# First expert weights and expert products in one block, with loads asked for early, staged inputs and one-hots in sets of two

## What is computed

```python
def peer(h, w_pq, sub_keys1, sub_keys2, u_table, v_table):
    ...
        q = (xb @ w_pq).reshape(PEER_BLOCK, PEER_HEADS, PEER_QDIM)
        ...
        v1, i1 = lax.top_k(s1, PEER_TOPK)
        v2, i2 = lax.top_k(s2, PEER_TOPK)
        ...
        top_s, sel = lax.top_k(cand, PEER_TOPK)
        eidx = jnp.take_along_axis(cidx, sel, axis=-1)
        g = jax.nn.softmax(top_s, axis=-1).astype(xb.dtype)
        act = jax.nn.gelu(jnp.einsum('thkd,td->thk', u_table[eidx], xb), approximate=False)
        return jnp.einsum('thk,thkd->td', g * act, v_table[eidx])
```

## Time and profile before

| | |
|---|---|
| Device time, median of 3 runs | 4201.07 us (4199.33 to 4202.46) |
| Time of the profiled execution | 4197.49 us |
| Its span, first to last instruction | 4195.7 us |
| TensorE busy | 3802.9 us, 91% |
| VectorE busy | 2992.6 us, 71% |
| ScalarE busy | 1232.7 us, 29% |
| GpSimd busy | 1747.3 us, 42% |
| Granted TensorE clock, mean | 0.932 of full speed |

### The profile page before, as it was taken

One profiled execution on the slowest core, in us unless ns is written; L12 is line 12 of the kernel. 1 busy time (PEld: TensorE's weight loads), 2 busy tenths in 40 slices (PEclk: granted clock), 3 DMA queues, 4 the chain that ended last, 5 costly groups with the idle time before them and its releaser, 6 DMA issues.

```text
span 4195.7 us, 58772 instructions
## 1 busy us (share of the span) xinstructions
PE 3802.9 (91%) x19146; PEld 3082.0 (73%) x19146; DVE 2992.6 (71%) x6028; ACT 1232.7 (29%) x1871; POOL 1747.3 (42%) x1065
## 2 busy tenths in 40 slices
PE   8899876999668999387999999999989999999998
PEld 1699843566555444166999999999979999999997
DVE  0322244333441999897999999998888888888888
ACT  0411033222222222074333333333223232332332
POOL 0222000000220233202565565555557777777775
PEclk9799977899779999657999999999999999999999
DMA  7388700566433111047999999999999999999997
GB/s 248 114 269 286 250 2 20 161 202 205 139 111 97 35 35 35 15 180 278 328 339 333 327 339 327 346 327 354 336 336 338 343 333 345 336 341 345 331 347 273
DMA packets 302319, 1018.03 MB, mean 243 GB/s; under 512 B 30394, under 2 KB 61916, under 8 KB 294932
## 3 DMA queue, kind: packets, MB, share of 16 engines
q1 hardware_dynamic: 155348, 489.04, 34.8%
q0 software_dynamic: 127584, 481.35, 31.5%
q10 hardware_dynamic: 19296, 46.67, 2.9%
...
## 4 chain that ended last, share of the span: by engine, by line
PE 52%; DVE 1%; DMA 0%; issue 0%; ACT 0%; DVEq 0%; POOLq 0%
PE p_y L2144 25%; PE p_a L2125 9%; PE p_a L2124 9%; PE p_a L2128 8%; PE next_pw L1752 2%; DMA h_lo<-h_spill 0%; DVE p_y L2110 0%; DVE h_lo L2096 0%; DVE rows L2066 0%; DVE h_rows L2079 0%; DVE h_rows L2102 0%; DVE h_hi L2094 0%; DVE x1g L2113 0%; ACT pairsT L1986 0%; DVE u_raw L2105 0%
## 5 line engine op out<-in xcount | busy, mean ns | idle before, releaser
L2013 POOL DMA_INDIRECT rows<-in_v,pairsT x384 | 763.2, 1987 | 276.3 <-DVE h_rows L2079 184.4
L2013 POOL DMA_INDIRECT rows<-u_rows,pairsT x384 | 632.9, 1648 | 477.0 <-DVE pairsT L2066 404.5
L2124 PE MATMUL p_a<-h_hi,u_hi 128*128 128x384 f32 x2048 | 688.7, 336 | 39.3 <-DVE h_lo L2096 38.0
L2125 PE MATMUL p_a<-h_lo,u_hi 128*128 128x384 f32 x2048 | 692.1, 338 | 0.0
L2144 PE MATMUL p_y<-v_hi,g_hi 128*128 128x512 f32 x1536 | 486.9, 398 | 0.0
L1981 ACT ACTIVATE v_hi<-v_raw 128x1024 fp32r<-128x1024 f32 x256 | 272.0, 1062 | 727.0 <-PE p_y L2144 714.1
L2144 PE MATMUL p_y<-v_lo,g_hi 128*128 128x512 f32 x1536 | 475.8, 391 | 0.0
L2079 DVE SCALAR_TENSOR_TENSOR h_rows<-rows,pairsT,h_rows 128x1024 f32<-128x1024 f32 x381 | 466.4, 1279 | 2.1 <-DMA rows<-in_v,pairsT 2.1
L2066 DVE CUSTOM_DVE_ANT_0 rows<-rows,h_rows 128x1024 f32<-128x1024 f32 x384 | 450.6, 1220 | 24.1 <-DMA rows<-u_rows,pairsT 23.9
L2124 PEld LDWEIGHTS p_a<-h_hi,u_hi 128*128 128x128 f32 x2048 | 386.2, 189 | 50.4 <-DVE h_lo L2096 38.7
L2128 PE MATMUL p_a<-h_hi,u_lo 128*128 128x384 f32 x2048 | 396.8, 334 | 0.5 <-DVE u_lo L2041 0.5
...
## 6 DMA issues: line engine op xcount, KB each, us to landing
...
```

Of the source, the lines that this page charges most:

```text
L2013: pool.indirect_dma_start(rows[s][n % SLOTS][:], None, (keep.u_rows, v_rows)[g], at).then_inc(rows_in[s][n % SLOTS], 16)
L2124: nc.tensor.matmul(p_a[:, 0:GT], u_hi[s][:, k, :], h_hi[:, k, :], start=k == 0, stop=False)
L2125: nc.tensor.matmul(p_a[:, 0:GT], u_hi[s][:, k, :], h_lo[:, k, :], start=False, stop=False)
```

## The change

- `stage_weights` is gone. Its steps run at the start of the block of `stage_experts`: SP first asks for `h_cols` (now in the `x1` buffers), then for `u` and `v` of `j` = 0 and 1, then stores the weight blocks; POOL first asks for `h_lo`, then the first six gathers, waits for all stores, and loads `w_ring` and `x1`; ScalarE makes the four splits and `h_hi` of the first group ahead of the weight steps; VectorE makes `h_lo` behind them. PSUM tiles are shared: the indices' and `h`'s transposes lie in `p_y`, the second bank of the weight steps is `p_a`.
- The input of the second group is loaded in turn 104 of the first to `h_next`, in the memory of `wt`, and split on VectorE right behind the last `weigh` of the first group.
- The last up product of a group finishes tile by tile (`y_tile`); VectorE multiplies each into `y` (`finished`), also in the memory of `wt`, so `p_y` is free for the next group after the multiplications; the additions (`added`) for the first group come in turn 2 of the second, their stores in turn 4 and the loads of `x1` for the second in turn 16, all on POOL's queue.
- Two ranks instead of one are treated in turns 4 and 8 of each group (`ranks_after`), so none is left behind the last turn.
- The one-hots of four tokens lie as two sets of two: `[set, key, token]` in place of `[key, token]`. VectorE's operations keep their number and size; TensorE reads one number in two.
- In `stage_scores` the sum of squares and the root stay ahead of `mix_columns`, the scaling goes behind it.

```diff
 
-            def norm(t):
+            def squares(t):
                 act.wait_ge(x1_full, t + 1)
 
                 nc.scalar.activation(xn[:], x1[:], ACT.Square, accum_out=st[:, 0:1]).then_inc(ss, 1)
                 act.wait_ge(ss, t + 1)
                 nc.scalar.activation(st[:, 1:2], st[:, 0:1], ACT.Sqrt, scale=1.0 / D, bias=keep.cols[:, 4:5]).then_inc(rms, 1)
+
+            def scaled(t):
                 act.wait_ge(rec, t + 1)
                 nc.scalar.activation(xn[:], x1[:], ACT.Copy, scale=st[:, 2:3]).then_inc(xn_full, 1)
 
@@ -1566,7 +1568,8 @@
             def before():
                 mix_columns(0)
                 mix_columns(1)
...
@@ -1578,9 +1581,11 @@
                 if not isinstance(t, int) or t >= 2:
                     exps(t - 2)
                 if projects:
-                    norm(t + 1)
+                    squares(t + 1)
                 if transposes:
                     mix_columns(t + 2)
+                if projects:
+                    scaled(t + 1)
...
-    B = 4
+    B, IN = 4, 2
+    SETS = B // IN
     STEPS = GROUP * P // B
     PER_BLOCK = BLOCK // B
-
-    def __init__(self, nc, sem, m, keep, banks, name, base, iota):
+    LEAD = 2
+
...
+        self.hot_i = [m.sb(f"hot_i{i}", [P, self.SETS, N_KEYS, self.IN], F16) for i in range(2)]
+        self.hot_j = [m.sb(f"hot_j{i}", [P, self.SETS, N_KEYS, self.IN], F16) for i in range(2)]
+        self.hot_w = [[m.sb(f"hot_w{i}{k}", [P, self.SETS, N_KEYS, self.IN], F16) for k in range(2)] for i in range(2)]
...
     def vector(self, dve, n, s):
 
         nc, keep = self.nc, self.keep
-        shape = [P, N_KEYS, self.B]
-        column = lambda x: x[:, bass.ds(n * self.B + self.base, self.B)].unsqueeze(1).to_broadcast(shape)
+        shape = [P, self.SETS, N_KEYS, self.IN]
+        column = lambda x: x[:, bass.ds(n * self.B, self.B)].rearrange("p (c b) -> p c b", b=self.IN).unsqueeze(2).to_broadcast(shape)
+        keys = self.iota.unsqueeze(1).to_broadcast(shape)
         dve.wait_ge(self.pw_full, n + 1)
-        nc.vector.tensor_tensor(self.hot_j[s][:], self.iota, column(keep.index[:, 1]), ALU.is_equal).then_inc(self.equal_full, 1)
-        nc.vector.tensor_tensor(self.hot_i[s][:], self.iota, column(keep.index[:, 0]), ALU.is_equal)
+        nc.vector.tensor_tensor(self.hot_j[s][:], keys, column(keep.index[:, 1]), ALU.is_equal).then_inc(self.equal_full, 1)
+        nc.vector.tensor_tensor(self.hot_i[s][:], keys, column(keep.index[:, 0]), ALU.is_equal)
         dve.wait_ge(self.equal_full, n + 1)
         for k in range(2):
             last = nc.vector.tensor_tensor(self.hot_w[s][k][:], self.hot_j[s][:], column(keep.parts[:, k]), ALU.mult)
         last.then_inc(self.hot_full, 1)
-    def tensor(self, pe, n, s):
+    def tensor(self, pe, n, s, banks):
+
         pe.wait_ge(self.hot_full, n + 1)
-        pe.wait_ge(self.pw_read, n + 1)
+        pe.wait_ge(self.pw_read, n + (self.LEAD + 1 - len(banks)))
...
+                last = self.nc.tensor.matmul(banks[s % len(banks)][:, b, :], self.hot_i[s][:, b // self.IN, :, b % self.IN],
+                                             self.hot_w[s][k][:, b // self.IN, :, b % self.IN], start=k == 0, stop=k == 1)
...
+    def store(self, eng, block, stored, ahead=0):
+
+        wait_count(eng, stored, (block - ahead) * 16)
         eng.sem_inc(self.wt_free, 1)
-        eng.wait_ge(self.pw_read, block * self.PER_BLOCK + (self.PER_BLOCK + self.banks))
+        eng.wait_ge(self.pw_read, block * self.PER_BLOCK + (self.PER_BLOCK + self.LEAD))
+        eng.dma_start(self.keep.w_dram[block], self.wt[:, block % 2]).then_inc(stored, 16)
...
+    wt_flat = w.wt[:].rearrange("p a k t -> p (a k t)")
+    h_next = wt_flat[:, 0:KD * GT].rearrange("p (k t) -> p k t", k=KD)
+    y = [wt_flat[:, i * D:(i + 1) * D] for i in range(GROUP)]
+    hs = [x1[s][:].rearrange("p (k c) -> p k c", k=KD) for s in range(SPARSE)]
+    pw = m.ps("pw", [P, w.B, N_KEYS])
+    one_bank = [pw[:]]
+    two_banks = [pw[:], p_a[:].rearrange("p (b k) -> p b k", b=w.B)]
+    p_idx = [p_y[0][:, 0, 0:DENSE_AT], p_y[0][:, 1, 0:DENSE_AT], p_y[1][:, 0, 0:DENSE_AT]]
+    p_h = p_y[2][:].rearrange("p b c -> p (b c)")
...
+    def ranks_after(j):
+
+        return min(J, j + 1 + (j >= 4) + (j >= 8))
+
+    def weight_steps(eng, body):
+        body(0, 0)
+        body(1, 1)
+        with eng.Fori(1, w.STEPS // 2) as k:
+            for s in range(2):
+                body(k * 2 + s, s)
+
...
-        rest(J - 2)
-        rest(J - 1)
...
+                def first():
+                    if g == 0:
+                        w.store(sp, 0, w.stored)
+                        with sp.Fori(1, BLOCKS) as b:
+                            w.store(sp, b, w.stored)
+
+                blocks(sp, g, load, lambda n, j, s: None, first)
...
+                def first():
+                    if g == 0:
+                        act.wait_ge(h_in, 16)
+                        nc.scalar.activation(h_hi[:], h_lo[:].bitcast(F32), ACT.Copy).then_inc(h_hi_full, 1)
+                        weight_steps(act, lambda n, s: w.scalar(act, n, s, two_banks))
...
+            def load_x1(g):
+                for i in range(GROUP):
+                    wait_count(pool, y_out[0][i], 16 * g)
+                    pool.dma_start(x1[i][:], keep.x1_dram[SPARSE + g * GROUP + i]).then_inc(x1_in[i], 16)
+
+            pool.dma_start(h_lo[:].bitcast(F32), keep.h2_dram[:, :, DENSE_AT:DENSE_AT + GT]).then_inc(h_in, 16)
+            pool.wait_ge(idx_done, 2)
...
+                for j in range(SLOTS):
+                    gather(g, j)
+                if g == 0:
+                    pool.wait_ge(w.stored, 16 * BLOCKS)
                 load_w(g, 0)
                 load_w(g, 1)
-
-                o = g * J
-                for j in range(SLOTS):
-                    gather(o + j)
+                if g == 0:
+                    pool.wait_ge(cols_turned, SPARSE)
+                    load_x1(0)
+                asked = SLOTS
                 for j in range(J):
-                    if j + SLOTS < J:
-                        gather(o + j + SLOTS)
+                    for n in range(asked, min(ranks_after(j) + SLOTS, J)):
+                        gather(g, n)
+                    asked = max(asked, min(ranks_after(j) + SLOTS, J))
                     if g < GROUPS - 1 and j < w.STEPS and j % w.PER_BLOCK == w.PER_BLOCK - 1:
-                        w.store(pool, j // w.PER_BLOCK)
+                        w.store(pool, j // w.PER_BLOCK + BLOCKS, w.stored_next, BLOCKS)
                     if j % JC == JC - 1 and j // JC + 2 < CHUNKS:
                         load_w(g, j // JC + 2)
+                    if g == 0 and j == w.STEPS + 8:
+                        pool.wait_ge(w.stored_next, 16 * BLOCKS)
+                        pool.dma_start(h_next, keep.h2_dram[:, :, DENSE_AT + GT:DENSE_AT + 2 * GT]).then_inc(h_in, 16)
+                    if g and j == 4:
+                        for i in range(GROUP):
+                            pool.wait_ge(y_full, i + 1)
+                            pool.dma_start(out_rows(SPARSE + i), x1[i][:]).then_inc(y_out[0][i], 16)
+                    if g and j == 16:
+                        load_x1(1)
...
+            def finished(g, i):
+                dve.wait_ge(y_tile, g * GROUP + i + 1)
+                nc.vector.tensor_mul(y[i], p_y[i][:].rearrange("p b c -> p (b c)"), keep.gate[:, 1, 1, :]).then_inc(y_mul, 1)
+
+            def added(g, i):
+                t = g * GROUP + i
+                dve.wait_ge(y_mul, t + 1)
+                dve.wait_ge(x1_in[i], 16 * (g + 1))
+                nc.vector.tensor_add(x1[i][:], x1[i][:], y[i]).then_inc(y_full, 1)
+
             for g in range(GROUPS):
+                def rest(j):
+                    for n in range(ranks_after(j - 1) if j else 0, ranks_after(j)):
+                        (dots, sums)[g](n)
+                    split_v(g * J + j + 2, j % 2)
+                    if g and j == 2:
+                        for i in range(GROUP):
+                            added(0, i)
+
+                def first():
+                    if g:
+                        dve.wait_ge(h_lo_full, g + 1)
+                        for i in range(GROUP):
+                            finished(0, i)
+                    split_v(g * J + 1, 1)
+
                 def between():
                     if g:
                         dve.wait_ge(rows_gelu, 1)
                         nc.vector.tensor_mul(keep.shares, keep.shares, keep.dots).then_inc(sums_done, 1)
                         dve.wait_ge(sums_done, 1)
 
-                def rest(j):
-                    (dots, sums)[g](j)
-                    if j + 2 < J:
-                        split_v(g * J + j + 2, j % 2)
-
-                dve.wait_ge(h_in, 16 * (g + 1))
-                nc.vector.tensor_copy(h_hi[:], h_lo[:].bitcast(F32)).then_inc(h_hi_full, 1)
+                raw = h_next if g else h_lo[:].bitcast(F32)
+                if g:
+                    dve.wait_ge(h_in, 32)
```

(40 more changed lines are left out.)

219 lines of the change are left out of this document (93 added, 126 removed).

## The result

| | before | after |
|---|---|---|
| Device time, median | 4201.76 us (4199.33 to 4202.82) | 4169.16 us (4161.68 to 4175.61) |
| Ratio after / before | | 0.9923 (95%: 0.9904 to 0.9942) |
| Profiled execution, time / span | 4197.49 / 4195.7 us | 4165.70 / 4163.9 us |
| TensorE, VectorE busy | 91%, 71% | 90%, 71% |
| Granted clock, mean | 0.932 | 0.933 |

A forecast was written before the change was run, and what follows sets the result against it. TensorE's down and up products bound the kernel: 4197.5 - 7 (block) - 15 (between groups) - 5 (end) + 3 (doubled ranks) - 35 (sets) = 4138.5 profiled, 4142 as median. Range 4127 to 4179.

The forecast's parts named there:

- Sets of two: One-hots in the weighted turns: fp16 products at 0.064 us, turn from 9.24 to 8.88 us, 35 us saved (0 to 40).
- rival (a): Weighted turns: reading is not what the fp16 products pay for, 35 of 59 us fall away, 4177; chance 0.28.
- The stops: Weighted turns of the first group: 3 us of stop, 0 to 7, from two ranks in turns 4 and 8.
- rival (b): Weighted turns: VectorE or the DMA engines hold the turn at 9.0 to 9.1 us, 4155 to 4165; chance 0.12.
- The doubled ranks: Turns 4 and 8: 3.4 us more VectorE work each; 3 us of stop in the first group, second group's lead covers it.
- The block: Weights and experts as one block: TensorE starts at about 1928, 7 us saved at the first up product (2 to 14).
- the first weights: Stage building the first weights: VectorE is the bound, so the one-hots in sets gain nothing there.
- rival (d): Block's start: loads, gathers and stores make the first eviction late, eating the whole hand-over; 4149; inside the forecast's chance 0.53.
- Between the groups: Hand-over from first to second group: TensorE's stop goes and the clock stays, 15 us saved (12 to 17).
- the end: Kernel's end: sparse sums done before, closing operations wait only for loads; 5 us saved (0 to 6).
- the scaling: Late scaling in the score stage: VectorE is the bound there, so 0 us saved (to 2).
- the likeliest case: Whole kernel: all terms as forecast, 4142 us; forecast band 4126 to 4154, with (d) in it, chance 0.53.

The follow-up runs named there:

- the pieces: The changed kernel with each 1.5 MB load of w_ring cut into six of 0.25 MB, one in each of six turns: 4142.10 us, ratio 0.9858.

## Why the prediction was right in its range and short in its size

**Sets of two: right, and a little better.** The turn was forecast at 8.88 us, it is 8.84. TensorE's price was put at 64 ns a product on the line of the 4-byte steps; it is 57 to 58. The three steps that are now measured at full clock are 118 ns (8 bytes), 57 (4 bytes) and 56 (2 bytes). At half clock it is 118, 107 and 107, and 107 ns is 128 / 1.2, one column a tick of that level. So the factor that the forecast leaned on, a pace that doesn't move with the clock, meant what it was taken for: the pace goes by the step of the operands, and rival (a) is wrong. The rule of the Trainium skill (SBUF — State Buffer, Door 1: The DMA port swizzle), by which an 8-byte step is read at full rate, doesn't hold for these products; the measurement decides. The rule of the Trainium skill (Vector Engine (DVE) Microarchitecture Reference, 5.2 Measured stream behaviour on trn2), that a port wants two adjacent 4-byte words, is not borne out by the token operand here, whose runs are two fp16 numbers, one such word: an operation stays at 0.42 us. With one number to a run it takes 0.68. By the Trainium skill (the same page, 5.1 Performance modes, the table) the doubled rate wants more than one element in the innermost dimension, and with that the trace agrees; which of its conditions failed there no run separates.

**The stops: the step that failed.** The forecast took the weighted turn as the largest of three mean loads (8.81, 8.6 to 8.7, 8.7) and added 0.07 us for their closeness; rival (b) did the same with 0.2. Both priced an even load. What happened is even in 85 turns of 96, which run at TensorE's pace, and a burst in the others: 22.3 us of stops where 0.07 x 96 + 3 = 10 were allowed. The rows had it in them: the DMA share of the earlier trace rows is a mean over 300 us, and a gather is asked for about two turns ahead of its use, a lead that at 9.24 us a turn just covered the 17 us that a held-up gather needs. In the kernel before VectorE waited 9.3 us for gathers in the whole weighted part and TensorE never saw it; the turn became 0.4 us shorter, and with it the lead, by an estimate, 0.8 us. Two runs show both halves of this: with the turn of 9.24 us again the stops of every eighth turn are gone, and so they are when the load is two turns apart from the store at 8.84.

**The doubled ranks: mis-sized.** 3 us (0 to 7) were forecast, in the first group alone. In the trace it is 10.3 us there (0.4 at the rank of turn 4, 9.9 at that of turn 8) and 3.0 in the second. They split in two: with the burst taken away, in two ways (the pieces, and the load two turns later), 5 us are left in the first group and 0.3 or less in the second. So half was the rank's own work in a turn with no room, as the forecast had it though with 3 us, and the other half again the burst, of the store and the load in turn 7. That the second group's lead covers them was wrong by those 3 us.

**The block: right at TensorE's start by luck, wrong behind it.** The first eviction is 2.3 us later than forecast. But the forecast said of the first weights that VectorE is the bound and nothing is gained by the sets, and that was wrong: a step took 1.381 us on the mean in the kernel before (the earlier trace rows show one of 1.37) and takes 1.344 now, 3.5 us in 96 steps. In both kernels the next `hot_j` starts 0.16 to 0.17 us behind the end of TensorE's eight products, which take 1.11 us before and 1.03 after; that points at a share of TensorE in the pace but doesn't prove it. The effect itself is shown: the kernel before with nothing but the sets starts its down products 3.5 us earlier, and with sets of four in the new order the step is 1.38 again. The two misses cancel, and TensorE starts within 0.5 us of the forecast. The read of the weights was put at 10 to 11 us from its issue and took 13.1; and the stop of 6.3 us costs clock: from 1948.7 to 1955 us the granted clock is 0.65 on the mean, so for part of the time at its 1.2 GHz level, where in the kernel before it is 1.00 from 1951 to 1955, and from the first up product to the third down product it takes 6.3 us in place of 4.1. What was forecast as 7 became 3.1, in the bounds of 2 to 14, and nearly all of it is the sets'. With sets of four the new order starts TensorE 10.5 us earlier than the kernel before (159.4 against 169.9, counted from the block's first DMA), the first up product 2.9 and the third down product 0.3: the result of rival (d), but lost behind TensorE's start, where it waits 7.4 us for the weights, and not at the first eviction. The pieces that are read as they are stored show what this read cost: 8.2 us at the third down product.

**Between the groups, the end, the scaling: right.** 14.7 against 15, though the margin was 0.4 us and not 1.1; 3.9 against 5; 0 against 0.

**The range and the chances.** The time, 4169, is in 4127 to 4179, but by luck: only rival (a), which is wrong, held the range open: the likeliest case's own bounds ended at 4154, rival (b)'s at 4165. What was missing was a case for bursts, with the price of one late gather for every load.
